# Attention of a hybrid diffusion layer: mask, scale and maximum in one VectorE instruction, heads in one sequence across query blocks, mixer products between heads

## The reference

```python
u = h @ w_in                                   # q (8 heads x 128), k, v (2 x 128 each), p (1024)
# latent tokens: query block of 128 reads 3 key blocks of its band and 4 blocks of cached context
s_loc = einsum(qb, kband) * HEAD_DIM**-0.5
s_loc = where(abs(kpos - qpos) <= 128 and inside, s_loc, -1e30)
s_ctx = einsum(qb, k_ctx) * HEAD_DIM**-0.5
p = softmax(concat([s_loc, s_ctx, sink]))
attn = p_loc @ vband + p_ctx @ v_ctx
# prompt tokens: the same without a mask over their own 2 key blocks
mixed = windowed_mean(p_group) - p_group       # windows 2, 4, 8, 16
pool = (mixed @ pool_w[g]) * pool_scale        # the "mixer", 4 groups of 256 columns
mix = concat([attn, pool]) @ w_out
x = x + g1 * mix
```

## Time and profile before

| what | value |
|---|---|
| median of 3 runs | 3696.39 us (3690.32 to 3703.71) |
| profiled execution | 3681.82 us, span of its instructions 3680.0 us |
| attention of chunk 0, from its first transposes to the output projection | 923 to 1108 us |
| attention of chunk 1 | 1305 to 1494 us |
| attention of chunk 2 | 1691 to 1785 us |
| output projections | 1108 to 1305, 1494 to 1691, 1785 to about 1900 us |
| expert loop | about 2020 to 3600 us |
| PE busy over the span | 3337.8 us (91%) |
| mean granted TensorE clock | 0.955 of full speed |

### The profile page before, as it was taken

The page is one execution under the profiler, slowest core; times in us unless marked ns, Lnnn a source line. Parts: engine busy times, 40 slices in busy tenths (PEclk is TensorE's granted clock), DMA queues, the critical chain, the costliest instruction groups (busy, mean ns, idle before and its releaser), DMA issues.

```text
span 3680.0 us, 52503 instructions
## 1 busy us (share of the span) xinstructions
PE 3337.8 (91%) x21052; PEld 3006.4 (82%) x21052; DVE 2169.9 (59%) x2375; ACT 1769.2 (48%) x1916; POOL 572.7 (16%) x611
## 2 busy tenths in 40 slices
PE   5899999997889989997759999999999999999991
PEld 4677777776768877786549999999999999999991
DVE  5634333453552245233787777777777777777774
ACT  5633433553552245223335555555555555555552
POOL 1054045002221013101210000000000000000001
PEclk9999999998999999998979999999999999999995
DMA  7765455586114411342558888888888888888876
GB/s 274 265 221 192 171 182 176 191 284 234 59 35 162 159 61 30 122 150 87 187 172 263 265 275 267 260 266 252 278 270 270 275 268 260 262 262 263 276 234 254
DMA packets 544952, 775.87 MB, mean 211 GB/s; under 512 B 16160, under 2 KB 409600, under 8 KB 536144
## 3 DMA queue, kind: packets, MB, share of 16 engines
q1 hardware_dynamic: 507072, 616.60, 50.2%
q0 software_dynamic: 37776, 157.84, 13.2%
HBM read 708.19 MB, written 66.19 MB: 210 GB/s over the span
## 4 chain that ended last, share of the span: by engine, by line
PE 75%; DVE 8%; ACT 5%; DMA 5%; POOL 4%; issue 3%; ACTq 0%; POOLq 0%; DVEq 0%
PE PS L787 29%; PE PS L789 12%; PE PS L571 12%; PE PS L743 10%; DVE wlo L1146 2%; PE PS L691 2%; ACT whi L860 1%; DMA arena_ab<-k_rope 1%; PE PS L662 1%; PE PS L710 1%; DVE lo_f L1425 1%; PE PS L518 1%; PE PS L665 1%; PE PS L678 1%; PE PS L519 1%
## 5 line engine op out<-in xcount | busy, mean ns | idle before, releaser
L787 PE MATMUL PS<-xT,hi_f 128*128 128x320 f32 x4096 | 1055.1, 346 | 0.0
L1425 DVE TENSOR_TENSOR lo_f<-raw_f,hi_f 128x2048 fp32r<-128x2048 f32 x384 | 878.9, 2289 | 255.2 <-ACT hi_f L1070 250.4
L789 PE MATMUL PS<-xT,lo_f 128*128 128x160 f32 x4096 | 965.9, 236 | 0.0
L1146 DVE TENSOR_TENSOR wlo<-raw,whi 128x2048 fp32r<-128x2048 f32 x204 | 471.8, 2330 | 661.2 <-ACT whi L860 660.7
L789 PEld LDWEIGHTS PS<-xT,lo_f 128*128 128x128 f32 x4096 | 782.3, 191 | 0.0
L1070 ACT ACTIVATE hi_f<-raw_f 128x2048 fp32r<-128x2048 f32 x384 | 733.0, 1909 | 96.9 <-PE PS L789 92.0
L787 PEld LDWEIGHTS PS<-xT,hi_f 128*128 128x128 f32 x4096 | 768.7, 188 | 0.0
L860 ACT ACTIVATE whi<-raw 128x2048 fp32r<-128x2048 f32 x204 | 387.3, 1916 | 538.9 <-PE PS L743 293.0
L787 PE MATMUL PS<-hid,hi_f 128*128 128x320 f32 x2048 | 533.7, 346 | 0.0
L789 PE MATMUL PS<-hid,lo_f 128*128 128x160 f32 x2048 | 482.8, 236 | 0.0
L789 PEld LDWEIGHTS PS<-hid,lo_f 128*128 128x128 f32 x2048 | 390.7, 191 | 0.0
(11 more groups left out here) (274 smaller groups left out, 4747.7 us busy)
## 6 DMA issues: line engine op xcount, KB each, us to landing
raw_f<-w_gate SPq DMA_DIRECT2D x128, 1024.0 KB, 4.9
raw_f<-w_up SPq DMA_DIRECT2D x128, 1024.0 KB, 5.0
raw_f<-w_down SPq DMA_DIRECT2D x128, 1024.0 KB, 5.1
raw<-w_ada SPq DMA_DIRECT2D x96, 1024.0 KB, 5.1
raw<-w_in SPq DMA_DIRECT2D x60, 1024.0 KB, 5.5
raw<-w_out SPq DMA_DIRECT2D x48, 1024.0 KB, 5.2
arena_ab<-x_sample POOLq DMA_DIRECT2D x8, 1024.0 KB, 12.0
arena_cd<-x_sample POOLq DMA_DIRECT2D x8, 1024.0 KB, 6.2
```

The costliest lines, as they stand in the source:

```text
L787: nc.tensor.matmul(PS[:, b + m, 0:2 * CAP], hi_f[:, n % NSPL_F, r, w], x, start=(kt == 0), stop=False, skip_group_check=True)
L789: ins = nc.tensor.matmul(PS[:, b + m, 0:CAP], lo_f[:, n % NSPL_F, r, w], x[:, 0:CAP], start=False, stop=(kt == last_kt), skip_group_check= ...
L1146: nc.vector.tensor_tensor(wlos[slot(n)], raws[slot(n)], whis[slot(n)].bitcast(F32), ALU.subtract).then_inc(lo_ok, 1)
L1425: nc.vector.tensor_tensor(lo_f[:, n % NSPL_F], raw_f[:, n % NRAW_F], hi_f[:, n % NSPL_F].bitcast(F32), ALU.subtract).then_inc(f_lo_ok, 1)
```

## The change

- The mask products are gone. The key blocks of a head are laid in the order left local block, 4 context blocks, middle, right (`key_blocks`), and the scores are computed in runs that are contiguous in `kT` and stay in one bank (`key_runs`): 4 products in place of 2 for most heads.
- A row pattern `band` (left mask, five blocks of zero, right mask; 128x896) stays in SBUF. One `tensor_tensor_reduce` takes scores and `band`, adds, multiplies by -SCALE, writes the result to `pp` and gives its minimum, at most minus the sink. It replaces `reduce_max` and `tensor_scalar`. The exp then reads `pp` (SBUF) in place of PSUM, with scale -1. The PSUM pair is free after this instruction (`masked`), not after the exp.
- The Q unit of the next block stands behind head 5 of the block before; there are two `qT` buffers (the second lies in `h2T`). The steps behind a head count heads, not units: an M or Q unit has no L691 and no L710 of its own. The M units stand behind heads (0,0), (1,3), (2,3), (3,5) in chunks 0 and 1, and (0,0), (0,4), (1,0), (1,5) in chunk 2.
- Chunk 2 has four slots for `pp`, `pT` and `sm`, transposes 3 heads behind and value products 4 behind; DVE alone copies to `pT` there.
- The two weight pieces are split in the M units 1 and 2. The output projection takes the pieces in the order 2, 3, 0, 1, so that the mixer's half comes first, and waits for `o_lo` only ahead of piece 0.
- The mixer result is written over `pin`; the two mask transfers move from POOL's first instructions to behind `load_q(0)`; `PE_PAD` is 95.

```diff
-PE_PAD = 64
+OUT_KG = (2, 3, 0, 1)
+PE_PAD = 95
...
+MIX_AT = [[(0, 0), (1, 3), (2, 3), (3, 5)], [(0, 0), (0, 4), (1, 0), (1, 5)]]
+LAG = [(1, 2), (3, 4)]
+SLOTS = (2, 4)
...
+        units.append((tc, "Q", 0, 0))
         for b in range(nt):
-            units.append((tc, "Q", b, 0))
             for h in range(NH):
                 units.append((tc, "H", b, h))
-            for g in range(b * per, b * per + per):
-                units.append((tc, "M", b, g))
+                if h == 5 and b + 1 < nt:
+                    units.append((tc, "Q", b + 1, 0))
+                if (b, h) in MIX_AT[cond]:
+                    units.append((tc, "M", b, MIX_AT[cond].index((b, h))))
...
+def key_blocks(tc, b):
     t0, nt, cond = CH[tc]
     if cond:
+        return [0, 1], P
+    q, first, cn = t0 + b, max(0, t0 - 1), PAST // P
+    left, mid, right = (cn + k - first if 0 <= k < ST else None for k in (q - 1, q, q + 1))
+    places = [left] + list(range(cn)) + [mid, right]
+    return [k for k in places if k is not None], P if left is None else 0
+
+def key_runs(places):
+    runs = []
+    for z, kb in enumerate(places):
+        if runs and z % 4 and kb == runs[-1][1] + runs[-1][2]:
+            runs[-1][2] += 1
+        else:
+            runs.append([z, kb, 1])
+    return runs
...
+        def attention_steps(tc):
+            n = heads_by(unit_end[tc]) - heads_by(unit_start[tc])
+            s = [(k, heads_by(k) - heads_by(unit_start[tc]) if kind(k) == "H" else None)
+                 for k in range(unit_start[tc], unit_end[tc])]
+            return s + [(None, n + z) for z in range(LAG[CH[tc][2]][1])]
...
                             if kind(k - 2) == "H":
-                                pe.wait_ge(exped, heads_by(k - 1))
+                                pe.wait_ge(masked, heads_by(k - 1))
...
-                            if cn:
-                                nc.tensor.matmul(flat[:, 0:cn * P], qT[:, h, :], kT[:, base:base + cn * P],
-                                                 start=True, stop=True)
-                            l0 = base + loc[0] * P
-                            last = nc.tensor.matmul(flat[:, cn * P:w], qT[:, h, :], kT[:, l0:l0 + len(loc) * P],
-                                                    start=True, stop=not (ml or mr), skip_group_check=True)
-                            if ml:
-                                last = nc.tensor.matmul(flat[:, cn * P:(cn + 1) * P], identr[:], maskr[:, 0:P],
-                                                        start=False, stop=not mr, skip_group_check=True)
-                            if mr:
-                                last = nc.tensor.matmul(flat[:, w - P:w], identr[:], maskr[:, P:2 * P],
-                                                        start=False, stop=True, skip_group_check=True)
+                            for z, kb, n in key_runs(key_blocks(tc, b)[0]):
+                                last = nc.tensor.matmul(flat[:, z * P:(z + n) * P], qTs[b % 2][:, h, :],
+                                                        kT[:, base + kb * P:base + (kb + n) * P], start=True, stop=True,
+                                                        skip_group_check=True)
...
-                pe.wait_ge(exped, heads_by(unit_end[tc]))
+                pe.wait_ge(masked, heads_by(unit_end[tc]))
                 pe.wait_ge(copied, copies_by(unit_end[tc]))
-                pe.wait_ge(o_lo, heads_by(unit_end[tc]) // 4)
-                pe.wait_ge(pt_a, heads_by(unit_end[tc]))
-                pe.wait_ge(pt_v, heads_by(unit_end[tc]))
...
+                        if cc == 0 and kg == 0:
+                            pe.wait_ge(o_lo, heads_by(unit_end[tc]) // 4)
...
+                        nc.scalar.activation(v, v, ACT.Exp, bias=sm[:, s, 1:2], scale=-1.0,
+                                             accum_out=sm[:, s, 2:3]).then_inc(exped, 1)
...
+                        if gi in (1, 2):
+                            split_hi()
...
-                            link(nc.vector.reduce_max(s[:, 0:1], flat[:, 0:w], AXX))
-                            nc.vector.tensor_scalar(s[:, 1:2], s[:, 0:1], -SCALE, sinks[:, 1, h:h + 1],
-                                                    ALU.mult, ALU.min).then_inc(masked, 1)
+                            dve.wait_ge(p_tr, through)
+                            nc.vector.tensor_tensor_reduce(out=pp[:, s, 0:w], in0=flat[:, 0:w], in1=band[:, m0:m0 + w],
+                                                           scale=-SCALE, scalar=sinks[:, 1, h:h + 1], op0=ALU.add,
+                                                           op1=ALU.min, accum_out=sm[:, s, 1:2]).then_inc(masked, 1)
...
+                            if h in (1, 2):
+                                split_lo()
...
-            dma(mask_in[:, 0:P], t["k_mask"][0]).then_inc(consts_in, 16)
-            dma(mask_in[:, P:2 * P], t["k_mask"][1]).then_inc(consts_in, 16)
...
             load_q(0)
+            dma(band[:, 0:P], t["k_mask"][0]).then_inc(band_in, 16)
+            dma(band[:, 6 * P:7 * P], t["k_mask"][1]).then_inc(band_in, 16)
```

More of the change, by code:

```diff
@@ L212, in hybrid_backbone_step @@
             for cc in range(4):
[L213 removed]
+                pieces += [piece(w_out, kg, cc * CC) for kg in OUT_KG]
         PS = ctx.enter_context(nc.psum_tensor("PS", [P, 8, 512], F32))
@@ L740, in _ @@
                             s = slice(m * P, (m + 1) * P)
+                            first, final = (place, r) == (0, 0), (place, r) == (3, KG - 1)
                             for z, (w, x) in enumerate(((ahi[:, kt, s], hi[:, r, :]), (alo[:, kt, s], hi[:, r, :]),
@@ L982, in _ @@
             for tc, (t0, nt, cond) in enumerate(CH):
-                for k in range(unit_start[tc], unit_end[tc] + 2):
-                    if tc:
+                lag_v = LAG[cond][1]
+                pp, pT = bufs(tc)
+                for k, j in attention_steps(tc):
+                    if tc and k is not None:
                         if k == turn_at(tc):
@@ L1029, in _ @@
-                    if in_chunk(k - 2, tc) and kind(k - 2) == "H" and UNITS[k - 2][3] % 4 == 3:
-                        _, _, b, h = UNITS[k - 2]
-                        act.wait_ge(pv_ok, heads_by(k - 2) + 1)
+                        if gi in (1, 2):
+                            split_hi()
+                    head = behind(tc, j, 1)
+                    if head and not cond:
+                        hc, (_, _, b, h) = head
+                        act.wait_ge(p_tr, hc + 1)
+                        act.wait_ge(pv_ok, slot_of(tc, hc)[1])
+                        nc.scalar.activation(pT[:, slot_of(tc, hc)[0], 0:4, :],
+                                             PS[:, 4, :].rearrange("p (a b) -> p a b", a=4), ACT.Copy).then_inc(pt_a, 1)
@@ L1032, in _ @@
+                    head = behind(tc, j, lag_v)
+                    if head and head[1][3] % 4 == 3:
+                        hc, (_, _, b, h) = head
+                        act.wait_ge(pv_ok, hc + 1)
                         nc.scalar.activation(ahi[:, h - 3:h + 1, b * P:(b + 1) * P],
                                              PS[:, 6 + h // 4, :].rearrange("p (a b) -> p a b", a=4), ACT.Copy).then_inc(o_hi, 1)
-                    if k < unit_end[tc] and kind(k) == "H":
-                        act.wait_ge(sum_ok, hc_now + 1)
-                        nc.scalar.activation(pp[:, hc_now % 2, 0:w_now], pp[:, hc_now % 2, 0:w_now], ACT.Copy,
-                                             scale=sm[:, hc_now % 2, 5:6]).then_inc(p_ok, 1)
+                    head = behind(tc, j, 1 if cond else 0)
@@ L1038, in _ @@
+                    if head:
+                        hc, (_, _, b, h) = head
+                        s = slot_of(tc, hc)[0]
+                        v = pp[:, s, 0:len(key_blocks(tc, b)[0]) * P]
+                        act.wait_ge(sum_ok, hc + 1)
+                        nc.scalar.activation(v, v, ACT.Copy, scale=sm[:, s, 5:6]).then_inc(p_ok, 1)
                 if tc == 2:
@@ L1295, in router_share, with share @@
                 nc.vector.tensor_tensor(a, a, rs2[:, 3, cs].unsqueeze(2).to_broadcast([P, nt, NE]), ALU.mult).then_inc(aff_ok, 1)
+            nc.vector.memset(band[:, P:6 * P], 0.0).then_inc(band_ok, 1)
+            dve.wait_ge(band_ok, 1)
+            dve.wait_ge(band_in, 32)
             for tc, (t0, nt, cond) in enumerate(CH):
-                for k in range(unit_start[tc], unit_end[tc] + 2):
-                    if tc:
+                lag_v = LAG[cond][1]
+                pp, pT = bufs(tc)
+                flat_t = PS[:, 4:6, :].rearrange("p a b -> p (a b)")
+                def share(head):
+                    s = sm[:, slot_of(tc, head[0])[0], :]
+                    dve.wait_ge(sank, head[0] + 1)
+                    link(nc.vector.tensor_tensor(s[:, 4:5], s[:, 2:3], s[:, 3:4], ALU.add))
+                    nc.vector.reciprocal(s[:, 5:6], s[:, 4:5]).then_inc(sum_ok, 1)
+                for k, j in attention_steps(tc):
```

(10 more changed lines are left out.)

206 lines of the change are left out of this document (92 added, 114 removed).

## The result

The changed kernel takes 3642.9 us (median of 4 runs, 3635.9 to 3645.9); the kernel before took 3693.4 beside it (median of 4). The ratio is 0.9854, its 95% interval 0.982 to 0.9887: 50 us less, where 69 were forecast. The time lies inside the range on record (3598 to 3663), 16 us above the predicted 3627. On the profiled executions it is 3642.58 against 3681.82, 39 less.

The account below looks back on a forecast made before the run. Steady heads were taken as PE-bound, with attention losing time at block ends, stage ends and in chunk 2. Terms -10 + 0 - 40 - 22 + 23 - 19.5 - 0.5 = -69 gave 3696 - 69 = 3627 us, range 3598 to 3663.

Parts of the forecast that it names:

- Mask products, -10: Wide heads on PE: dropping the mask products takes a steady head from 4.05 to 3.85 us; net -10 us.
- The new DVE instruction, 0: Heads on DVE: the combined pass takes 1.3 us, about what it removes, and does not delay PE; 0 us.
- rival A: Heads: the DVE instruction runs at half rate, or ACT and DVE together bound them; +28 us, 3655 in all; chance 0.15.
- Block ends, -40: Ends of blocks in chunks 0 and 1: idle time and half clock go as heads run on; -40 us.
- stage ends, -22: Ends of attention chunks 0 and 1: lost time goes and the projection no longer starts cold; -22 us.
- M units among heads, +23: Chunks 0 and 1: M units 1 and 2 stall 3.5 us plus 1.2 for half clock, others less; +23 us.
- Rival C: Each M unit among heads costs 7 us, as a block end does now, and keeps the clock low; 3661; chance 0.09.
- Chunk 2, -19.5: Attention chunk 2: POOL's mixer chain sets the end, and earlier, separated M units bring the projection forward; -19.5 us.
- Start, -0.5: Kernel start: two transfers leave POOL's first issues, and 31 more empty instructions lie under PE's wait; -0.5 us.
- rival D: Expert loop: it slows down as the code before it changes length; at 6 us an expert +27, 3723; chance 0.03.
- E: Whole kernel: no gain, because a later stage waits for something that is not moved; chance 0.04.
- B: Stalls at M units are hidden or the clock does not fall, so most of the +23 goes; 3608; chance 0.17.

Follow-up runs that it names:

- e5: The changed kernel with the output projection's weight pieces back in the old order 0, 1, 2, 3; 3648.1 us, ratio 0.9902.
- e12: The kernel before with only the projection's new weight-piece order and the late wait for `o_lo`; 3683.4 us, ratio 0.9988.
- e3: The changed kernel with the rest of chunk 0's router work, done in attention chunk 1, four units later on ACT and DVE; 3643.0 us, ratio 0.9877.
- e11: e10 with mixer unit 0 of chunks 0 and 1 behind head (0,3) instead of (0,0); 3628.6 us, ratio 0.9833.
- e7: The changed kernel with POOL beginning mixer 1 of chunk 2 ahead of its wait for the store of `x1`; 3635.8 us, ratio 0.9874.
- e2: The changed kernel with 64 empty PE instructions at the start instead of 95; 3643.8 us, ratio 0.9878.
- e1: The kernel before with 95 empty PE instructions at the start instead of 64; 3687.1 us, ratio 0.9997.
- e10: The changed kernel with e7's edit and, in chunks 0 and 1, DVE's split half after the head behind mixer units 1 and 2; 3635.6 us, ratio 0.986.

## Why the prediction was right, and where it was off

*Mask products, -10: right.* 4.05 became 3.85, as written.

*The new DVE instruction, 0: right.* 1.23 us where 1.3 was taken, in place of the 1.30 + 0.04 of the earlier trace rows. Half rate, rival A, is refuted. The rule weighed there (the Trainium skill, page "Vector Engine (DVE) Microarchitecture Reference", section "Points that are easy to get wrong") speaks of two SBUF sources; with one source in PSUM the rows show full rate (1.15 us, where the maximum alone took 1.09), and no run here shows both in SBUF with an accumulator.

*Block ends, -40, and stage ends, -22: the gaps went.* The step over a query unit costs 0.6 us beyond a head, the stage's end has two waits of 0.74 where 0.4 and 0.7 were written, the projection starts at full clock (65.33 where 65.4 was written). But I gave the projection's new order a share in this that e5 and e12 don't find.

*M units among heads, +23: the step that failed.* In units 1 and 2 a stall of 3.01 us where 3.5 was written, and the half clock behind three of the four. But from 987.95 four more passes have begun only at 1013.75: 25.80 us. Four heads of 3.85, the unit's 3.4 and the queries' 0.9 leave 6.1 lost, not 4.7; counted alike the other three units lose 6.9, 4.9 and 6.7. So the step is mis-sized by some 1.4 on the mean, some 6 us in four units. In the first of them the half clock is the rest: 14 products, 7 transposes and 8 of the queries took 3.35, 1.70 and 1.63 us in place of 1.73, 0.93 and 1.04, 3.0 in all, where 1.2 was written. In the second the clock stayed full, and more waits came on top, the longest 1.53 us, which the prediction has no term for. The sum of a head's denominator (L1330), 0.15 us elsewhere, stood still until POOL's instruction ended, and PE waited for the scaling behind it:

```profile
1044.46 6.39 POOL L1707 TENSOR_TENSOR arena_cd<-arena_cd 128x1050 f32<-128x1050 f32 x3
1048.68 2.19 DVE L1330 TENSOR_TENSOR sm<-sm 128x1 f32<-128x1 f32 x1
1052.20 0.98 PE L734 MATMUL PS<-ident,arena_cd 128*128 128x128 f32 x7 [1.53 <-ACT arena_cd L1061]
```

The kernel before has the same at each of the six block ends of the wide chunks, also ahead of the 3.76 us of idle time of the earlier trace rows, in which my sum saw only the block's end:

```profile
1015.43 1.44 DVE L1361 TENSOR_TENSOR sm<-sm 128x1 f32<-128x1 f32 x1 [1.35 <-ACT sm L1008]
```

What this wait is worth in either kernel no run shows by itself. The larger part of the miss is mixer unit 0 of chunk 1; my sum has 2.4 us for the units 0 of both wide chunks. It brought 3.80 us of wait (ACT's router squares, above) and, since mixer 1 begins once it is done, the collision with the router: 7.44 more and a half clock. e3 gets back 6 of that, e11 11. Rival C's 7 us for each unit is nearer to these than my 4.7 and the 1.2 of a unit 0; its total, 3661, lies 18 above the measured time as mine lies 16 below.

*Chunk 2, -19.5: right in its mechanism, -17.3.* The mixer chain was written as M 1 from 1718.5, which is 27.7 behind the stage's start at 1690.8; measured 31.3. Then 16 and 18 us to the next units; measured 17.1 and 15.6. e7 shows that the residual load I let stand ahead of mixer 1 is 5 us of the stage.

*Start, -0.5.* "The 31 more empty instructions lie under that wait" is wrong: they end at 15.47, the wait at 13.48 (e2). It costs nothing measurable.

*The loop, rival D: refuted.* PE is busy 1565 of 1650 us in both kernels. The 3 us of the tail lie in projection 2 and what follows it; the stretch from its first product to the loop's first (150.9 before, 153.6 after) was between 151.7 and 156.2 in the other runs, so they are no cost of the change. E is refuted by the gain, B by the stalls.

The sum against the profiled pair, -69 against -39: the wide chunks' attention -44 written (all terms for them but the 4.6 of warmer projections), -27 measured; the first two projections -4.6 and -7.5; chunk 2 -19.5 and -17.3; front -0.5 and +9.7; the tail 0 and +3. So 17 of the 30 us are the mixer units' term (6 and 11, as above), and 13 are front and tail, which differ as much between kernels with the same code there. The stage lengths that I wrote beside the sum, 158 and 163, claimed 7 us more than its terms give. On medians, where the front's chance falls out for the most part, the gain is 50.

Left open: why the front takes 923 in one execution and 943 in another (its granted clock in the first 200 us differed, but no run tells cause from effect), the part of the heads' pipelining alone, and how much of the 7 us of a block's end was POOL's hold on DVE.

## What to carry to other kernels

When a unit of work is moved between pipelined ones, ask what its end releases on the other engines, and what those then run beside: here the moved unit 0 cost less than what its early end let loose. Place side work (a weight split) where the time is set by an engine that has no part in it; the same two splits were free under POOL's chain and cost 11 us at the stage's end. And before a stage's difference is explained, look at how much that stage differs between kernels that share its code.

## What was not expected of the hardware

Small DVE instructions stand still while a GpSimd element-wise instruction runs: 0.17 us become 1.68 and 1.79, 0.23 become 2.13 and a head's 0.15 become 2.19, each ending within 0.1 us of GpSimd's. TENSOR_TENSOR, TENSOR_SCALAR and a COPY within SBUF (L1301, 1.13 us) did; RECIPROCAL and TENSOR_REDUCE did not, nor did the pass with one input in PSUM, here in chunk 0:

```profile
1050.94 2.64 POOL L1712 TENSOR_TENSOR arena_cd<-arena_cd 128x512 f32<-128x512 f32 x2
1052.11 1.14 DVE L1354 CUSTOM_DVE_ANT_0 arena_cd<-PS,arena_cd,sinks 128x896 f32<-128x896 f32 x1
```

The Trainium skill, page "SBUF — State Buffer", section "SBUF: two separate sides", says that the two engines share a port pair that whichever starts first holds for its whole instruction, and that DVE needs it for two inputs in SBUF or in a two-port mode. The trace agrees in each of these rows, and I had not weighed it.

An empty instruction of PE that raises a semaphore costs at most 15.47 / 95 = 0.16 us (e1 and the changed kernel, the issue of the first transposition included).

The same stall of 3.01 us was followed by the half clock three times in four in the changed kernel and fifteen times in sixteen in e2, e3, e5 and e7, and the shorter one of 2.38 (e10) four times in four.
